# Prompt attention with the values as the stationary operand: outputs stacked by head and turned, without the copy and the transposition

## The reference, cut to what matters

```python
z = jnp.einsum('bqhd,bshd->bhqs', q, k) * SB_SCALE
log_keep = jnp.where(valid, log_sigmoid(-z), 0.0)        # valid: key before query
log_rest = cumsum(log_keep, axis=3, reverse=True) - log_keep
a = jnp.where(valid, exp(log_sigmoid(z) + log_rest), 0.0)
o = jnp.einsum('bhqs,bshd->bqhd', a, v)
...
h = x + jnp.concatenate([o_a, o_b], axis=-1) @ w_out
```

## Time and profile before

| what | us |
|---|---|
| median of three runs | 2021.91 (2019.43 to 2022.35) |
| the profiled execution | 2018.16 |
| its span, first to last instruction | 2016.4 |
| prompt attention loop, from about 425 to 619.5 | about 194 |
| two full groups of 16 steps in it | 43.91 each |

### The profile page before, as it was taken

How to read it: one execution, slowest core, us unless ns; L and a number is a source line. 1 busy time by engine, 2 the same in 40 slices (tenths; PEclk the granted TensorE clock), 3 DMA queues, 4 the chain that set the end, 5 groups by cost and what they waited for, 6 DMA issues and landing times.

```text
span 2016.4 us, 29545 instructions
## 1 busy us (share of the span) xinstructions
PE 1848.8 (92%) x12726; PEld 1744.4 (87%) x12726; DVE 796.2 (39%) x1015; ACT 514.7 (26%) x943; POOL 630.0 (31%) x337
## 2 busy tenths in 40 slices
PE   5999999989998538888899999999999999999998
PEld 4989989977775237777799999999999999999898
DVE  5551215567883346565511522212122222214432
ACT  4221122246664313434211310000101010103211
POOL 4133313313440111211343433443433443432330
PEclk9999999999999759888889999999999999999999
DMA  5121312120004433433133111111111111111121
GB/s 163 43 72 37 106 64 85 49 69 24 1 1 127 114 99 81 122 81 104 36 87 84 42 43 53 43 42 53 42 43 53 43 42 53 42 42 52 58 70 45
DMA packets 197599, 126.51 MB, mean 63 GB/s; under 512 B 38960, under 2 KB 190916, under 8 KB 197476
## 3 DMA queue, kind: packets, MB, share of 16 engines
q1 hardware_dynamic: 188048, 111.69, 19.2%
q10 hardware_dynamic: 9428, 13.02, 1.8%
HBM read 100.07 MB, written 24.62 MB: 62 GB/s over the span
## 4 chain that ended last, share of the span: by engine, by line
PE 76%; DVE 11%; issue 6%; ACT 3%; DMA 2%; POOL 0%; SPq 0%; ACTq 0%; DVEq 0%; POOLq 0%
PE psum L1999 40%; PE psum L1831 8%; PE psum L2316 4%; PE psum L1800 3%; PE psum L1801 3%; PE psum L1802 3%; PE psum L1887 2%; PE psum L1864 2%; PE psum L2135 2%; DVE act_lo_plain L1471 1%; DVE area L1569 1%; PE psum L2034 1%; PE psum L1876 1%; PE psum L2335 1%; DVE area L1413 1%
## 5 line engine op out<-in xcount | busy, mean ns | idle before, releaser
L1999 PE MATMUL psum<-act_hi,w_round 128*128 128x352 f32 x1920 | 369.9, 326 | 0.4 <-DVE act_lo L1703 0.4
L876 POOL TENSOR_TENSOR w_round<-w_plain,ones 128x1024 fp32r<-128x1024 f32 x80 | 178.2, 2227 | 531.8 <-DMA w_plain<-in_w_up_dram 230.8
L1999 PEld LDWEIGHTS psum<-act_hi,w_round 128*128 128x128 f32 x1920 | 321.8, 190 | 1.3 <-DVE act_lo L1703 0.7
L1999 PE MATMUL psum<-hid_hi,w_round 128*128 128x352 f32 x1344 | 260.0, 324 | 0.4 <-DVE hid_lo L1733 0.4
L1999 PEld LDWEIGHTS psum<-hid_hi,w_round 128*128 128x128 f32 x1344 | 224.9, 188 | 0.7 <-DVE hid_lo L1733 0.7
L1710 DVE TENSOR_TENSOR area<-psum,area 128x1056 f32<-128x1056 f32 x72 | 90.5, 1257 | 312.2 <-PE psum L1999 312.1
L1999 PE MATMUL psum<-act_lo,w_round 128*128 128x352 f32 x960 | 208.0, 325 | 0.0
L877 POOL TENSOR_TENSOR w_round<-w_plain,w_round 128x1024 fp32r<-128x1024 f32 x80 | 195.8, 2447 | 6.3
L1332 ACT ACTIVATE hid_hi<-area 128x1056 fp32r<-128x1056 f32 x28 | 30.5, 1088 | 592.5 <-DVE area L1726 592.5
L1800 PE MATMUL psum<-w_round,act_hi 128*128 128x256 f32 (+1 forms) x576 | 166.2, 289 | 6.7 <-POOLq L835 3.6
L1999 PEld LDWEIGHTS psum<-act_lo,w_round 128*128 128x128 f32 x960 | 164.4, 189 | 0.0
(11 more groups left out here) (296 smaller groups left out, 3000.6 us busy)
## 6 DMA issues: line engine op xcount, KB each, us to landing
w_plain<-in_w_up_dram SPq DMA_DIRECT2D x32, 512.0 KB, 4.1
w_plain<-in_w_down_dram SPq DMA_DIRECT2D x32, 512.0 KB, 3.4
w_plain<-in_w_in_dram SPq DMA_DIRECT2D x14, 1024.0 KB, 5.5
conv_scratch<-area ACTq DMA_DIRECT2D x12, 512.0 KB, 2.7
w_plain<-decay_scratch SPq DMA_DIRECT2D x9, 512.0 KB, 3.7
area<-t_scratch SPq DMA_DIRECT2D x9, 512.0 KB, 4.2
area<-x_scratch SPq DMA_DIRECT2D x9, 512.0 KB, 5.6
area<-in_x_prompt_dram SPq DMA_DIRECT2D x8, 512.0 KB, 3.3
```

Source lines behind the costliest of these rows:

```text
L876: own.link(pool.tensor_tensor(hi, ring_raw(n), ones[:, 0:1].to_broadcast([P, RB]), ALU.mult))
L1999: last = pe.matmul(bank(bank_set(tile) + c)[:, 0:CH], w(k), a(k)[:, CH * c:CH * (c + 1)], start=(begins and k == ks[0] and w is w_h and a ...
```

## The change

The stationary and the moving operand of `values` change places: 64 columns of the values are loaded, and 128 columns of turned weights move. The result has the head's 64 features on the partitions (the lower half of them for u = 0, the upper for u = 1) and the block's 128 tokens along the row, which is how `act_hi` and `act_lo` hold it. `turn_out` and its semaphore go, as does the buffer `o_tok`; ACT rounds from PSUM straight into `act_hi`, where the copy was, and DVE only subtracts, where it rounded and subtracted.

```diff
-            def copy_out(t):
+            def round_out(t):
                 act.wait_ge(o_ready, 1 + 2 * t + 2)
-                act.activation(o_tok[:, t % 2, :], bank(6 + t % 2)[:, 0:P], ACT.Copy).then_inc(o_copied, 1)
+                act.activation(act_hi[:, WT + t // NT, P * (t % NT):P * (t % NT + 1)], bank(6 + t % 2)[:, 0:P],
+                               ACT.Copy).then_inc(o_rounded, 1)
...
-            def split_out(t):
-                dve.wait_ge(o_turned, t + 1)
-                src = bank(6 + t % 2)[:, P:2 * P]
+            def rest_of_out(t):
+                dve.wait_ge(o_rounded, t + 1)
                 k, cols = WT + t // NT, slice(P * (t % NT), P * (t % NT + 1))
-                own.link(dve.tensor_copy(act_hi[:, k, cols], src))
-                own.link(dve.tensor_tensor(act_lo[:, k, cols], src, act_hi[:, k, cols].bitcast(F32), ALU.subtract))
-                dve.sem_inc(o_split, 1)
+                dve.tensor_tensor(act_lo[:, k, cols], bank(6 + t % 2)[:, 0:P], act_hi[:, k, cols].bitcast(F32),
+                                  ALU.subtract).then_inc(o_split, 1)
...
-            def turn_out(t):
-                pe.wait_ge(o_copied, t + 1)
-                pe.transpose(bank(6 + t % 2)[:, P:2 * P], o_tok[:, t % 2, :], ident[:]).then_inc(o_turned, 1)
...
-                    last = pe.matmul(bank(6 + t % 2)[:, HD * u:HD * (u + 1)], turned_buf[u][:, P * n:P * (n + 1)], v,
+                    last = pe.matmul(bank(6 + t % 2)[HD * u:HD * (u + 1), 0:P], v, turned_buf[u][:, P * n:P * (n + 1)],
                                      start=(n == 0), stop=(n == t % NT))
...
                 values(y)
-                if y % 2 and y >= 3:
-                    turn_out((y - 3) // 2)
-            turn_out(STEPS // 2 - 1)
```

More of the change, by code:

```diff
@@ L224, in trunk_step @@
         o_ready = sem("o_ready")
-        o_copied = sem("o_copied")
-        o_turned = sem("o_turned")
+        o_rounded = sem("o_rounded")
         o_split = sem("o_split")
@@ L371, in trunk_step @@
         turned_buf = (act_hi_plain[:, DEEP * TP:(DEEP + 1) * TP], act_lo_plain[:, DEEP * TP:(DEEP + 1) * TP])
-        o_tok = carve(area, tok0 + W, 2, P)
         at_buf = carve(area, tok0 + 2 * SW, 2, TP)
@@ L1088, in _ @@
                 if y and y % 2 == 0:
-                    copy_out(y // 2 - 1)
+                    round_out(y // 2 - 1)
                 if y == LAST_CONV + 2:
                     conv_outputs(NC - 1)
-            copy_out(STEPS // 2 - 1)
+            round_out(STEPS // 2 - 1)
             act.wait_ge(cs_stored, 1 + 32 * NC)
@@ L1473, in _ @@
                 if y % 2 and y >= 5:
-                    split_out((y - 5) // 2)
+                    rest_of_out((y - 5) // 2)
                 if y == LAST_CONV:
                     conv_taps(NC - 1, (NC - 1) % 2)
-            split_out(STEPS // 2 - 2)
-            split_out(STEPS // 2 - 1)
+            rest_of_out(STEPS // 2 - 2)
+            rest_of_out(STEPS // 2 - 1)
             for g in range(2):
```

## The result

The changed kernel takes 2024.36 us (median of 20 runs, 2021.53 to 2027.88), the kernel before 2020.27 us beside it (20 runs, 2015.8 to 2024.75). The ratio is 1.0023, with a 95% interval of 1.0015 to 1.003: slower by some 4 us. The direction was forecast, the size was not: I had said 2035 us, 13 us more than before, and the time lies under the low end of my range (2025). Of the 10.6 us between forecast and time, 1.6 lie in the base: I added to 2021.91 us, the median of three runs, and that of 20 is 2020.27. The other 9 or so are in the sum.

What follows compares the result with a forecast made beforehand. PE was taken to bound the loop, with DVE close behind. Run ends of +21.8 and +0.5 us, less 3.2, 5.0 and 0.6, gave +13.5 us: 2035 us against a base of 2021.91, range 2025 to 2044.

Steps and rivals of the forecast that it cites:

- The mechanism: At both ends of each values run, changing the array's form drains PE; the next load starts about 0.2 us late.
- 5.0 taken back: In the loop behind 460 us, PE wins back 5 of 5.9 us idle time (between 3 and 6) as DVE's load falls.
- the check with 42.69 us of PE work: Middle group: 42.69 + 16 x 0.39 - 8 x 0.11 = 48.0 us of PE work against 43.91, so +4.1 each.
- Per run +0.39 us: Both ends of each values run: ten passes take 1.555 us against 1.17; 56 runs behind 460 us give 21.8 us.
- The transposition of the outputs: Removed on PE: 32 transpositions of 0.11 us, 29 of them counted, so 3.2 us come off.
- No gain and no loss inside a run: Pace of value passes on PE: between 0.109 and 0.112 us a pass in the new form, 0.112 before.
- The 0.6 us at the end: End of the loop: the last output needs one transposition and one rounding less before the next stage, saving 0.6 us.
- the slack: Stretch up to 460 us, PE idle 11 of 35 us: of 3.1 us for eight runs' ends, 0.5 booked (0 to 3.1).
- the bounds I named: 0.37 to 0.41 us a run, 3 to 6 us taken back, 0 to 3.1 in the slack: 2031 to 2041 us.
- No price at the ends: Rival: changing form at the ends of values runs costs nothing; some -7 us, 2015 us; chance 0.11.
- Two halves side by side: Rival: value passes of both array halves overlap, DVE then bounds, the loop loses 25 us, 1997 us; chance 0.02.
- The clock: Rival: new PE gaps bring the granted clock to 0.86 in three later groups, +7.8 us each, 2058 us; chance 0.08.

Runs made afterwards that it cites:

- full form with one piece: Changed kernel with 128 value columns loaded, both halves written to the same bank columns, first head's output of each pair left out: 2008.45 us, ratio 0.9938.
- three passes more: Kernel before, with three more identity transpositions on PE ahead of each run of two or more value passes: 2028.79 us, ratio 1.0041.
- late subtraction: Changed kernel, with DVE's subtraction of each output made to wait until PE finished the values two steps later: 2024.32 us, ratio 1.0021.
- the two kernels with the extra pass: Changed kernel plus one 128-column pass per run of two or more value passes: in its middle, 2046.39 us; ahead of it, 2027.33 us.
- the pairs: Changed kernel, with an even and the next odd step's values issued together, halves alternating: 2012.69 us; with ACT's sigmoids ahead of its copies again, 2003.17 us.
- pairs that are not mixed: Changed kernel, with an even and the next odd step's values issued together, one half after the other: 2018.52 us, ratio 0.9992.

## Why the prediction was off, step by step

**The mechanism held.** Each run starts 0.20 us behind the last transposition and the scores start 0.20 us behind the last pass, as worked out from the earlier trace rows; the chain in a middle group is PE throughout; DVE's wait for the transposed output is gone (one wait of 0.9 us for ACT's rounding is left in a group); no wait of PE for DVE is listed in the middle groups; the clock stays at 1.00 in them. The direction followed from this. The size did not: two terms of the sum were mis-sized, and both made the forecast too long.

**The first step that failed is the size of "5.0 taken back".** I read the time that PE could win back from its idle time in the earlier trace rows, 1.22 us a group, and made the check with 42.69 us of PE work. But a pass that lasts 0.27 us and is followed by the next 0.11 us later is still counted as busy for a while after PE has nothing new to start, so short waits disappear in the busy row. The Trainium skill says (Trainium Kernel Development and Optimization, "Performance Expectations") that matmul busy time is a bad metric of how near a kernel is to its limit, because matmuls are pipelined; it does not say that waits hide in it. The runs agree with the warning. In the changed group no wait of PE for DVE or ACT is listed; taking off 16 run ends at 0.33 (5.3 us), and putting back eight transpositions at 0.06 (0.5 us) and the slower pace (0.4 us), leaves 41.45 us for PE's own work before. From the full form with one piece it is 41.25 + 0.5 = 41.75, an upper bound, since its busy row can hide waits too. So PE had 2.2 to 2.5 us of waiting in a group of 43.91, and all of it was used up.

The starts in the two traces show where it was. I measure a step from the last transposition of weights ahead of one run of values to the last one ahead of the next. Eleven of the 16 steps of a middle group are longer than before, by 0.30 to 0.32 us where no output's transposition went and by 0.24 to 0.28 us where one did. The other five, three of them with runs of two, four and six passes and two with runs of 14, are unchanged or up to 0.44 us shorter. Had they grown like the rest, the group would be 2.6 us longer: that is what PE waited there before, 1.4 us more than its row shows as idle. The experiments show what uses it up: a longer PE alone takes 1.4 us (three passes more), a DVE that is lighter and released earlier most of it (one piece), and the earlier release adds nothing once PE is longer (late subtraction).

**The second step that failed is "Per run +0.39 us".** In the sum for the ten-pass run I booked 0.11 us from the scores' load to the scores. Here is such a run in PE's timeline of the changed kernel:

```profile
597.85 0.71 PE L1869 MATMUL psum<-ident,act_hi_plain 128*128 128x128 f32 x5
598.49 1.30 PE L1881 MATMUL psum<-act_hi_plain,area 128*64 128x128 f32 x10
599.73 1.12 PE L1861 MATMUL psum<-area 128*128 128x512 f32 x2
```

The last transposition starts at 597.85 + 0.71 - 0.27 = 598.29 us, the values 0.20 us later as forecast, and the scores 1.44 us after that transposition, where it was 1.17 and I had 1.555. The scores' first pass starts with its load. Only 0.05 us more pass until their second one, so a run of ten costs 0.32 us, as the whole steps above say: 0.07 us less than forecast, 4 us over 56 runs. The 0.33 us of the two kernels with the extra pass are the ends without what the pace gives back.

**The transposition of the outputs was worth less.** I booked 0.11 us for each. By the steps above (0.25 against 0.31 to 0.32 us for runs of like length) it was worth 0.06 to 0.07. Over 29 of them my sum was 1.3 us too kind to the change.

**"No gain and no loss inside a run"** was a gain of 0.0025 us a pass: up to the first pass of the scores, a run of four is 0.281 us longer than before and one of 16 is 0.251. Over the 536 passes of the 56 runs behind 460 us that is 1.3 us; my 0.39, with nine passes at 0.11 against 0.112, had most of it in already.

**The 0.6 us at the end did not come.** From the scan of step 62 to the next stage's first pass it takes 13.86 us now (611.30 to 625.16) and took 13.38 before (606.27 to 619.65). The timeline of the changed kernel there:

```profile
623.50 0.28 ACT L1063 ACTIVATE act_hi<-psum 128x128 fp32r<-128x128 f32 x1 [2.07 <-PE psum L1881]
623.67 0.68 ACT L1098 ACTIVATE area<-area,halves 128x128 f32<-128x128 f32 x2
623.80 0.29 DVE L1460 TENSOR_TENSOR act_lo<-psum,act_hi 128x128 fp32r<-128x128 f32 x1 [2.05 <-ACT act_hi L1063]
624.25 0.30 ACT L1100 ACTIVATE area<-area 128x128 f32<-128x128 f32 x1
624.45 0.61 ACT L1101 ACTIVATE v_s<-area 32x512 f32<-32x512 f32 x1
625.13 0.11 PEld L1937 LDWEIGHTS psum<-ident,gc_all 128*72 128x72 f32 x1 [1.92 <-issue]
```

DVE is through with the last output at 624.09 us, but the next stage also needs what ACT stages for it (lines 1098 to 1101), queued behind the last rounding on ACT. That chain ends at 625.06 us. In the trace of before it ended at 619.55 us, level with DVE's last subtraction (619.47), so making DVE's chain shorter could win next to nothing.

**The account, by stretches.** My sum of 13.5 us, divided: three middle groups at 4.1 (12.3), some 1.9 ahead of them (0.5 in the slack, four run ends of 0.39 less 0.2 for transpositions) and the rest, -0.7, behind them. The traces show 3 x 1.94 = 5.8, -1.0 and +0.5, together 5.3 us. (By the bounds I named, 0.37 a run, 6 taken back and nothing in the slack, the low end of the forecast is 2033 us and not the 2031 I wrote; the time lies under both.) In a group 2.2 us are missing: 16 x 0.07 = 1.1 to 1.2 by the runs, pace included; 1.4 by the waits under the busy row as read from the five steps (0.9 to 1.2 by the other two estimates, 42.69 less 41.75 or 41.45); and 8 x 0.045 = 0.4 the other way by the transpositions. That is 2.1 to 2.2, or 1.6 to 2.0 by the other estimates. Behind the groups 1.2 us were lost against the forecast, the end and its idle time. Ahead of them 2.9 us are missing, and that I can't divide: from the first scan to that of step 14 the loop took 45.38 us before (429.13 to 474.51) and takes 44.37 now (429.37 to 473.74). Both traces have a spell at the lower of the clock's two levels there (a granted clock of 0.50 from 460 to 462 us, behind 4 us in which PE was busy for 1.8 us before and 1.4 us after). The kernel with the late subtraction was as idle there (busy for 1.3 of the same 4 us), has no such spell after 452 us, and needs 43.50 us for the same steps (429.69 to 473.19); so a part is probably the clock's, and differs from run to run.

**The rivals.** No price at the ends: refuted, 0.33 us are there in each. Two halves side by side: not in the change but for its last two runs, as argued; the pairs show that it is real when the passes alternate. The clock: 1.00 in the middle groups.

## What to carry to other kernels

A gain that is read from the idle time of an engine whose passes overlap can be too low: here PE's rows showed 1.22 us a group and 2.2 to 2.6 were there. Count the engine's starts at their steady pace and book the difference to the length as waiting, since added work falls into it first and a lighter partner takes it back too. A narrow form that is entered for one half of the array at a time paid its two ends here, 0.33 us, and won next to nothing inside a run; it paid when the passes of both halves were issued in turn (3.1 us a group less than before), and then the order on the engines that feed it (here ACT's sigmoids ahead of its copies) was worth another 1.5 us a group.

## What the runs showed of the hardware

At the very end of the loop in the changed kernel, where no scores stand between the last two runs of values, the passes of the two halves came in turn though they had been issued one run after the other. Six rows of PE's timeline there:

```profile
621.60 0.27 PE L1881 MATMUL psum<-act_hi_plain,area 128*64 128x128 f32 x1
621.66 0.27 PE L1881 MATMUL psum<-act_lo_plain,area 128*64 128x128 f32 x1
621.71 0.27 PE L1881 MATMUL psum<-act_hi_plain,area 128*64 128x128 f32 x1
621.77 0.27 PE L1881 MATMUL psum<-act_lo_plain,area 128*64 128x128 f32 x1
621.82 0.27 PE L1881 MATMUL psum<-act_hi_plain,area 128*64 128x128 f32 x1
621.88 1.58 PE L1881 MATMUL psum<-act_lo_plain,area 128*64 128x128 f32 x13
```

The overlap lasts for three passes of the first run, then the second runs alone at its 0.11 us. The pairs that are not mixed show the same where their two runs of 16 meet (531.09 to 531.37 us): three passes of the first run in turn with the second. A pass of 128 columns in the full form, of the kind that adds the mask, cost 0.06 us when it was put between the transpositions and the values (46.65 against 45.85 us in 14 runs), about half of the 0.11 us that each of the three transpositions took in the same place.
